# Feed-forward parts taken straight from x, low weights on VectorE, reordered casts and sums, and decay levels on half blocks, in a two-block model on one core

## What is computed

```python
# HGRN2: o_t = sum over s <= t of (q_t * decay(s..t)) . key_s * i_s
log_f = jnp.log(lb + (1.0 - lb) * sig)
b = jnp.cumsum(log_f)                       # h_dec in the kernel
scores[t, s] = sum_k q[t, k] * key[s, k] * exp(b[t, k] - b[s, k])   # s <= t
# residual, norm, feed-forward
x = x + merged @ w_out[layer]
h2 = rms_norm_2(x, norm2_g[layer])
x = x + (jax.nn.silu(h2 @ w_ffn_gate[layer]) * (h2 @ w_ffn_up[layer])) @ w_ffn_down[layer]
```

## Time and profile before

| what | value |
|---|---|
| median of three runs | 1315.31 us (1315.01 to 1316.07) |
| time of the profiled execution | 1316.15 us |
| its span, first to last instruction | 1314.3 us |
| granted TensorE clock, mean | 0.998 |
| TensorE busy | 1278.6 us |
| VectorE busy | 841.4 us |
| ScalarE busy | 695.5 us |
| GpSimd busy | 118.8 us |

### The profile page before, as it was taken

One profiled execution on the slowest core, in us unless ns is written; L12 is line 12 of the kernel. 1 busy time (PEld: TensorE's weight loads), 2 busy tenths in 40 slices (PEclk: granted clock), 3 DMA queues, 4 the chain that ended last, 5 costly groups with the idle time before them and its releaser, 6 DMA issues.

```text
span 1314.3 us, 24944 instructions
## 1 busy us (share of the span) xinstructions
PE 1278.6 (97%) x10572; PEld 1146.2 (87%) x10572; DVE 841.4 (64%) x1257; ACT 695.5 (53%) x901; POOL 118.8 (9%) x77
## 2 busy tenths in 40 slices
PE   6999999999999999999999999999999999999997
PEld 5998989889999999998888888999999899788885
DVE  3667856876656977667655545556978657655542
ACT  2556546865766566244544434766566344544432
POOL 0000000000001320222000000000440131000000
PEclk9999999999999999999999999999999999999999
DMA  9866746624444433235455554434433225455452
GB/s 385 294 234 263 291 181 234 224 97 161 151 137 148 147 130 123 67 106 183 164 188 188 172 189 156 161 129 161 160 130 130 66 85 188 163 190 187 166 178 78
DMA packets 35103, 222.94 MB, mean 170 GB/s; under 512 B 3888, under 2 KB 8240, under 8 KB 9264
## 3 DMA queue, kind: packets, MB, share of 16 engines
q1 hardware_dynamic: 31248, 216.23, 46.7%
q10 hardware_dynamic: 3744, 5.11, 1.2%
HBM read 220.28 MB, written 1.05 MB: 168 GB/s over the span
## 4 chain that ended last, share of the span: by engine, by line
PE 83%; DVE 9%; ACT 4%; DMA 2%; issue 1%; SPq 0%; POOL 0%; ACTq 0%; DVEq 0%
PE pj L617 55%; PE yv L617 13%; PE sc L617 10%; PE tp L617 4%; DVE ring_rounded L731 3%; DMA ring<-weights 2%; ACT w_split L722 1%; DVE hT L2048 1%; PE tp L486 1%; PE tp L1849 1%; DVE xT L989 1%; DVE att_area L560 1%; DVE rw L1637 0%; DVE big L1812 0%; ACT att_area L516 0%
## 5 line engine op out<-in xcount | busy, mean ns | idle before, releaser
L731 DVE TENSOR_TENSOR ring_rounded<-ring,w_split 128x2048 fp32r<-128x2048 f32 x108 | 256.2, 2376 | 53.0 <-ACT w_split L722 50.7
L722 ACT CAST w_split<-ring 128x2048 fp32r<-128x2048 f32 x106 | 201.7, 1904 | 31.2 <-PE pj L617 22.0
L2065 DVE TENSOR_TENSOR ring_rounded<-ring,big_rounded 128x2048 fp32r<-128x2048 f32 x62 | 142.2, 2293 | 102.8 <-ACT big_rounded L1946 102.8
L617 PE MATMUL pj<-h_split,w_split 128*128 128x256 f32 x1264 | 173.8, 288 | 0.5 <-DVE h_split L2445 0.3
L617 PE MATMUL pj<-h_split,ring_rounded 128*128 128x256 f32 x1264 | 164.4, 280 | 1.1 <-DVE ring_rounded L731 1.1
L617 PEld LDWEIGHTS pj<-h_split,w_split 128*128 128x128 f32 x1264 | 157.5, 190 | 8.4 <-issue 6.0
L617 PEld LDWEIGHTS pj<-h_split,ring_rounded 128*128 128x128 f32 x1264 | 155.2, 188 | 2.7 <-DVE ring_rounded L731 1.9
L1946 ACT CAST big_rounded<-ring 128x2048 fp32r<-128x2048 f32 x66 | 125.9, 1908 | 51.7 <-PE pj L617 50.1
L617 PE MATMUL pj<-hT_rounded,w_split 128*128 128x256 f32 x1136 | 148.0, 283 | 0.0
L617 PEld LDWEIGHTS pj<-hT_rounded,w_split 128*128 128x128 f32 x1136 | 141.5, 192 | 0.0
L1318 POOL TENSOR_TENSOR big<-big 128x512 f32<-128x512 f32 x16 | 31.1, 1941 | 727.0 <-DVE big L1251 714.9
(11 more groups left out here) (368 smaller groups left out, 2220.3 us busy)
## 6 DMA issues: line engine op xcount, KB each, us to landing
ring<-weights SPq DMA_DIRECT2D x180, 1024.0 KB, 4.9
big<-weights SPq DMA_DIRECT2D x20, 1024.0 KB, 7.7
first_block<-biases ACTq DMA_DIRECT2D x26, 192.0 KB, 4.4
first_block<-biases SPq DMA_DIRECT2D x6, 192.0 KB, 10.9
xT<-x_t SPq DMA_DIRECT2D x1, 1024.0 KB, 9.6
out_t<-scr SPq DMA_DIRECT2D x4, 256.0 KB, 2.9
con<-constants SPq DMA_DIRECT2D x1, 897.0 KB, 6.6
aux<-small SPq DMA_DIRECT2D x1, 832.0 KB, 10.8
```

Of the source, the lines that this page charges most:

```text
L617: return nc.tensor.matmul(out, lhsT, rhs, start=start, stop=stop, skip_group_check=True)
L722: act.post(nc.scalar.copy(w_split[:, w % 2], ring[:, in_ring(idx)]), s["w_high"])
L731: dve.post(nc.vector.tensor_tensor(ring_r[:, at], ring[:, at], w_split[:, w % 2].bitcast(F32), ALU.subtract), s["w_low"])
L2065: e.tell(engine.tensor_tensor(w_low(t, i), w, value(w_high(i)), ALU.subtract), signal)
```

## The change

- *Feed-forward h.* The scaled copy of x in `hT` is dropped. ScalarE makes the high parts of h directly from x with a scale, ahead of the square; VectorE makes the low parts from x, gain and high part in one instruction. VectorE also makes the low weights of the first two feed-forward slots, the first ahead of the last residual and the second behind it, and the low parts of the third pair of h move ahead of the first. `pool_ffn` goes.
- *Even mixer's end.* ScalarE casts the next high weights ahead of waiting for the evacuation; VectorE's low part of the odd mixer's first slot moves behind the last residual; two of the dummy products go.
- *Start of each layer.* The norm's sums stand between the fourth and the fifth of u's low parts instead of ahead of them all.
- *Decay levels.* q is made for the upper halves of the blocks only and packed into 256 columns; the key is written for the lower halves only (for level 7 and level 6 all of it); the products have 64 moving columns each; the merge copies the upper halves only.

```diff
@@ -878,11 +878,12 @@
...
                 products(high, u_high, k, k == 0)
                 products(low, u_high, k)
-            if layer == 0:
-                pe_second_sums(pe, 3)
-            else:
-                pe_down_sums(pe)
             for k in range(KC):
+                if k == KC // 2:
+                    if layer == 0:
+                        pe_second_sums(pe, 3)
+                    else:
+                        pe_down_sums(pe)
                 pe.take(s["u_low"])
                 last = products(high, u_low, k, False, k == KC - 1)
@@ -1133,6 +1134,21 @@
...
         ORDER = [LEVELS] + list(range(LEVELS - 1, -1, -1))
 
+        half_of = lambda ap, n, x: ap.rearrange("p (a x n) -> p a x n", x=2, n=n)[:, :, x]
+        h_upper = lambda i: flat(h_qf[i % 2])[:, 0:SEQ]
+
+        def pe_level(banks, k, q, signal):
+
+            for T in range(NT):
+                for c in range(2):
+                    for half in range(2):
+                        rows = slice(half * HD, (half + 1) * HD)
+                        at = 2 * T + c
+                        last = matmul(banks[half][:, at * HD:(at + 1) * HD], k[rows, c, T * P:(T + 1) * P],
+                                      q[rows, (2 * c + T) * HD:(2 * c + T + 1) * HD])
+                        if at == 3:
+                            last.then_inc(signal.sem, 1)
+
         def pe_hgrn(pe, layer):
             fill(pe, pe_slot, f"hgrn{layer}", -1)
@@ -1140,17 +1156,18 @@
...
                 pe.take(s["hgrn_q"])
                 pe.take(s["hgrn_k"])
-                q, k = h_qf[i % 2], h_kf[i % 2]
+                q, k = h_upper(i), h_kf[i % 2]
                 if l == LEVELS:
                     for c in range(2):
                         for r in (0, HD):
-                            last = matmul(tp[r // HD][:, c * P:(c + 1) * P], k[r:r + HD, c, 0:P], q[r:r + HD, c, P:SEQ])
+                            last = matmul(tp[r // HD][:, c * P:(c + 1) * P], k[r:r + HD, c, 0:P],
+                                          q[r:r + HD, c * P:(c + 1) * P])
                     last.then_inc(s["hgrn_cross"].sem, 1)
                     fill(pe, pe_slot, f"hgrn{layer}", i)
...
                 if i > 1:
                     pe.take(s["hgrn_merged"], 2)
-                pe_by_half((h_bank(i, 0), h_bank(i, 1)), k, q, s["hgrn_scores"])
+                pe_level((h_bank(i, 0), h_bank(i, 1)), k, q, s["hgrn_scores"])
                 fill(pe, pe_slot, f"hgrn{layer}", i)
                 if i == 3:
@@ -1255,7 +1272,9 @@
...
         def dve_hgrn_q(dve, i):
             dve.take(s["hgrn_factor"])
-            dve.tell(nc.vector.tensor_tensor(flat(h_qf[i % 2]), flat(hq), flat(h_d[i % 2]), ALU.mult), s["hgrn_q"])
+            n = 1 << ORDER[i]
+            dve.tell(nc.vector.tensor_tensor(h_upper(i).rearrange("p (a n) -> p a n", n=n), half_of(flat(hq), n, 1),
+                                             half_of(flat(h_d[i % 2]), n, 1), ALU.mult), s["hgrn_q"])
 
         def dve_hgrn(dve, layer):
@@ -1281,9 +1300,11 @@
...
                 for T in range(NT):
                     dve.take(s["hgrn_scores"])
-                    dve.tell(nc.vector.copy_predicated(flat(h_sc[T]).rearrange("p (h t) -> p h t", t=P),
-                                                       level(l).bitcast(I32).unsqueeze(1).to_broadcast([P, NH, P]),
-                                                       quarters(h_bank(i, T))), s["hgrn_merged"])
+                    n, blocks = 1 << l, P >> (l + 1)
+                    into = flat(h_sc[T]).rearrange("p (h a x n) -> p h a x n", h=NH, x=2, n=n)[:, :, :, 1]
+                    mask = half_of(level(l), n, 1).bitcast(I32).unsqueeze(1).to_broadcast([P, NH, blocks, n])
+                    dve.tell(nc.vector.copy_predicated(into, mask, h_bank(i, T)[:, 0:SEQ].rearrange(
+                        "p (h a n) -> p h a n", h=NH, n=n)), s["hgrn_merged"])
             if layer == 1:
                 dve.do(nc.vector.tensor_tensor(v_diff, vfirst[:, :, :], r_v, ALU.subtract))
@@ -1329,7 +1350,8 @@
...
             if i >= 3:
                 pool.take(s["hgrn_scores"], 4 if i == 3 else 2)
-            pool.tell(nc.gpsimd.tensor_tensor(flat(h_kf[i % 2]), flat(h_key), flat(h_d[i % 2]), ALU.mult), s["hgrn_k"])
+            lower = lambda ap: flat(ap) if i < 2 else half_of(flat(ap), 1 << ORDER[i], 0)
+            pool.tell(nc.gpsimd.tensor_tensor(lower(h_kf[i % 2]), lower(h_key), lower(h_d[i % 2]), ALU.mult), s["hgrn_k"])
 
 
@@ -1869,7 +1891,7 @@
...
                     pe_sums_by_token(pe)
                 products(h_low, w)
-                pe.take(s["ffn_low_first"] if i < 2 else s["ffn_low"])
+                pe.take(s["ffn_low"])
                 products(h_high, low).then_inc(slot_done, 1)
                 if i == 0:
@@ -2039,17 +2061,27 @@
...
                          s["final_second"])
 
-        def dve_residual_split(dve, stem, g_at):
+        def dve_residual_split(dve, t, g_at):
+
+            stem = t + "out"
+
+            def h_low_pair(i):
+
+                for k in (2 * i, 2 * i + 1):
+                    dve.take(s["h_high"])
+                    dve.post(nc.vector.scalar_tensor_tensor(hT_r[:, k], xT[:, k], vec[:, g_at + k:g_at + k + 1],
+                                                            value(h_high[:, k]), ALU.mult, ALU.subtract), s["h_low"])
 
             for i in range(KC // 2 + 1):
                 if i < KC // 2:
+                    if i == KC // 2 - 1:
+                        h_low_pair(i - 1)
+                        weight_low(dve, t, 0)
                     dve_residual(dve, stem, slots=(i,))
-                    for k in (2 * i, 2 * i + 1):
-                        dve.post(nc.vector.tensor_scalar(hT[:, k], xT[:, k], vec[:, g_at + k:g_at + k + 1], None,
-                                                         ALU.mult), s["h_to_split"])
-                if i:
-                    for k in (2 * i - 2, 2 * i - 1):
-                        dve_h_low(dve, h_high, k)
+                if i == KC // 2:
+                    weight_low(dve, t, 1)
+                if i and i != KC // 2 - 1:
+                    h_low_pair(i - 1)
                 if i < KC // 2 - 2:
                     dve_lows(dve, IDX[f"{stem}{i + 2}"])
@@ -2058,21 +2090,20 @@
...
             dve.tell(nc.vector.reciprocal(token_scale, rt[:, 0:2]), s["token_scale"])
 
-        def weight_low(engine, e, t, i, signal):
+        def weight_low(dve, t, i):
 
             w = ring[:, in_ring(w_at(t, i))]
-            e.take(s["ffn_high"])
-            e.tell(engine.tensor_tensor(w_low(t, i), w, value(w_high(i)), ALU.subtract), signal)
+            dve.take(s["ffn_high"])
+            dve.tell(nc.vector.tensor_tensor(w_low(t, i), w, value(w_high(i)), ALU.subtract), s["ffn_low"])
 
         def dve_ffn(dve, t):
-            dve.take(s["ffn_high"], 2)
             for j in range(FC // 2):
-                weight_low(nc.vector, dve, t, 2 * j + 2, s["ffn_low"])
+                weight_low(dve, t, 2 * j + 2)
                 if j:
                     dve_ffn_split(dve, j - 1)
                 else:
                     dve_token_scale(dve)
-                weight_low(nc.vector, dve, t, 2 * j + 3, s["ffn_low"])
+                weight_low(dve, t, 2 * j + 3)
                 for T in range(NT):
                     dve.take(s["ffn_silu"])
@@ -2080,15 +2111,10 @@
...
                         dve.do(ins)
                 dve.tell(ins, s["ffn_hidden"])
-            weight_low(nc.vector, dve, t, FC + 2, s["ffn_low"])
+            weight_low(dve, t, FC + 2)
             dve_ffn_split(dve, FC // 2 - 1)
             for i in range(FC + 3, FFN_SLOTS):
-                weight_low(nc.vector, dve, t, i, s["ffn_low"])
-
-        def pool_ffn(pool, t):
-            for i in range(2):
-                weight_low(nc.gpsimd, pool, t, i, s["ffn_low_first"])
-            pool.take(s["ffn_high"], FFN_SLOTS - 2)
+                weight_low(dve, t, i)
 
 
@@ -2251,7 +2277,6 @@
...
             for n in ODD_GATE:
                 pe_slot(pe, n)
-            pe_turning(sc[0], 2)
             pe_squares(pe, KC // 2 - 1, scr)
             pe_turning(sc[0], 3)
@@ -2346,9 +2371,9 @@
...
                     act_highs(act, IDX[ODD_FIRST[0]])
                     nc.scalar.preload_act_table(ACT.Sqrt)
+                act_highs(act, min(IDX[f"even_out{i}"] + 2, IDX["even_out3"]))
                 evacuated(act, f"even_out{i}")
                 act_square(act, i, scr)
-                act_highs(act, min(IDX[f"even_out{i}"] + 2, IDX["even_out3"]))
             act_sums_copy(act)
             act_root(act)
@@ -2387,9 +2412,10 @@
...
                         nc.scalar.preload_act_table(ACT.Sqrt)
                     evacuated(act, f"{t}out{i}")
+                    for k in (2 * i, 2 * i + 1):
+                        act.post(nc.scalar.activation(h_high[:, k], xT[:, k], ACT.Identity,
+                                                      scale=V("norm2", 8 * layer + k)), s["h_high"])
```

(8 more changed lines are left out.)

2 lines of the change are left out of this document (1 added, 1 removed).

## The result

The changed kernel takes **1307.27 us** (median of four runs, 1307.01 to 1308.1) against 1315.36 (1315.01 to 1316.07): a ratio of 0.9939 with a 95% interval of 0.9922 to 0.9956, 8.1 us less. The prediction was 1306.6 us, in a range of 1301.2 to 1309.6. The profiled execution took 1307.17 us.

A forecast was written before the change was run, and what follows sets the result against it. TensorE, busy 97% of the span, was taken to bound the kernel, so only its waits or work could yield gain. Terms 4.0 + 2.3 + 0.9 + 1.5 = 8.7 us gave 1315.3 - 8.7 = 1306.6 us, range 1301.2 to 1309.6.

The forecast's parts named there:

- Feed-forward, 4.0 forecast: Start of both feed-forwards: slots 0 and 1 fall from 14.16 to 12.1 us, gaining 2.0 us a layer.
- no gain, and no price: Feed-forward: removed scalings and new form of h's parts are hidden by TensorE's 5.5 us a slot, worth nothing.
- Even mixer, 2.3 forecast: Even mixer's end: earlier high casts gain 1.0 us, the moved low cast 1.3, the removed dummies nothing of their own.
- moving VectorE's low cast behind the last residual ... gain 1.3: Even mixer's end: the residual starts at about 188.25 instead of 189.74, squares' sums at 190.1 instead of 191.46.
- The first term: Even mixer's end: ScalarE's high cast ahead of the evacuation removes TensorE's 0.99 us wait at even_out2, gain 1.0.
- Start of each layer, 0.9 and 0 forecast: Layer starts: low-part products moved ahead of the norm's sums fill second-layer waits, 0.9 us; first layer 0.
- Decay levels, 1.5 forecast: Decay levels, both layers: 0.7 us from shorter products, 0.5 from a key's wait, 0.3 from shorter merges.
- shorter merges return about 0.15 us a layer: End of the decay levels: TensorE's loads wait 0.33 us for the last merge; halved merges return part of it.
- Columns pace the levels: Rival, decay levels: moving columns set the pace, adding 5.3 us of gain, 1301.3 us; chance 0.12.
- The feed-forward gives back: Rival, feed-forward: VectorE's residual comes over 1.0 us late, TensorE waits at the squares, 4.0 lost, 1310.6 us; chance 0.09.
- The waits only move: Rival, all stages: TensorE stands as long at the next producer in each place, 1314 us; chance 0.05.
- GpSimd pays by runs: Rival, decay levels: keys in short runs take up to 6.2 us and hold up products, 1322.8 us; chance 0.05.

The follow-up runs named there:

- ff_gpsimd: Changed kernel with the first two low weight parts of each feed-forward back on GpSimd, direct parts of h kept: 1309.33 us.
- ff_h_by_hT: Changed kernel with h's parts made the old way (scale into hT, square, cast, subtract), low weights still on VectorE: 1306.85 us.
- even_low_first: Changed kernel with VectorE's low part of the odd mixer's first slot back ahead of the even mixer's last residual: 1307.63 us.
- sums_first: Changed kernel with the norm's sums ahead of all eight low-part products again at both layers' starts: 1307.91 us.
- level_pace: Changed kernel with narrower decay-level products, 32 moving columns in the first layer, 64 stationary in the second; work left out, times only: 1304.31 us.
- fine_levels_early: Changed kernel with the decay levels in the order 7, 6, 5, 1, 0, 4, 3, 2: 1307.18 us.

## Why the prediction was right

- **What bounds the kernel.** Right. 97% of the span was TensorE, and the gain lay in its marked waits and in their neighbourhood, not in the 50 us that the other two engines were spared.
- **Feed-forward, 4.0 forecast, 3.54 measured.** Right in mechanism: VectorE takes the parts in 2.29 each, in time for TensorE, and ff_gpsimd shows that giving them back costs 2.2 us. The term was 0.46 too large. I put slots 0 and 1 at 12.1 us, the steady 11.51 and 0.57 more; they take 0.9 more than the steady ones. The small groups are not the reason: 0.57 for the squares' sums and 0.36 for the sums by token, in place of 0.36 for the turning, are the 0.57 that I added. Of the other 0.3, 0.1 is the price of the direct form, and 0.2 lies in products beside the groups: the eight ahead of the squares' sums take 1.97 us (1.88 in the steady slots) and the eight behind the sums by token 1.94 (1.81), a cost of the change of kind that I put at nothing. ff_gpsimd also shows that the 4.0 were not GpSimd's instructions alone: 1.3 us of the gain stay when it makes the parts. The sentence that the form of the parts is hidden, "no gain, and no price", was almost right: ff_h_by_hT shows a price of 0.1 a layer, because a chain of slightly longer ScalarE work makes the high weights 0.6 us later. The first low weights had 1.5 us of slack where I put 2.0, the squares 1.0, as forecast.
- **Even mixer, 2.3 forecast, 2.69 measured.** The sum holds, its split does not. The step that failed is "moving VectorE's low cast behind the last residual ... gain 1.3". With the casts moved, this edit is worth nothing (even_low_first, -0.07); the casts alone bring all of the 2.7 us, where I gave them 1.0. I read the position of the low part in the trace of before and did not carry the first edit's 2 us of earlier casting through the queues to the second. The first term was 1.16, not 1.0: the mark of a wait counts from the modelled end of the matmul before, and starts to starts give more. That the dummies would stand in the way was right, with 0.63 us.
- **Start of each layer, 0.9 and 0 forecast, 0.81 and 0 measured.** Right, and sums_first gives the same 0.80.
- **Decay levels, 1.5 forecast, 1.18 measured.** The pace by the load was right to the last digit shown: 1.16 to 1.11 us, loads at 0.97. So was the key's wait (0.5). The keys took 0.99 to 1.11 us where I put 0.9. The step that failed is "shorter merges return about 0.15 us a layer": they returned nothing. The merges of the last two levels did not get shorter (1.53 and 1.51 us a pair, 1.55 and 1.52 before), and the wait behind them was not theirs.
- **The rivals.** Columns pace the levels: refuted by the 1.11 us and again by level_pace. The feed-forward gives back: the squares were there 1.0 us ahead. The waits only move: each stage kept its gain. GpSimd pays by runs: it does, by 0.12 us at the finest two levels, where the rival needed over 2.7. The spread of the subtraction from 1.05 to 3.08 us, which I took as a sign for it, has nothing to do with runs: GpSimd was held up by VectorE (fine_levels_early).
- **The closeness of the sum.** 8.7 forecast, 8.2 by stages, 8.1 by medians. The terms missed by -0.46, +0.39, -0.09 and -0.32, so a part of it is luck: the even mixer's surplus, from the term whose split was wrong, covers nearly half of what the others lack.

## What to carry to other kernels

When several edits act on one stretch, price them in the order in which they act, with each queue's new times carried forward: two edits that both "remove" a wait can be one gain. Before a shape is halved, ask which operand sets the pace: here the stationary columns did, and the cheap half was the wrong one. A wait's mark names the last semaphore; whether that binds shows only when it comes earlier and the wait stays.
